# The first projection in four groups of 396 to 412 streamed columns, in another order of columns

## The chip, the core and the metric

The kernel runs on one core of a Trainium2 chip. The metric is the device time of one execution in microseconds, of which three runs are shown. Beside them stands one execution that the hardware profiler recorded. TensorE multiplies (PE in the profile; PEld is its loading of the stationary operand), ScalarE (ACT) rounds weights, moves results out of PSUM and computes exponentials and logarithms, VectorE (DVE) does the elementwise work, GpSimd (POOL) a few small steps, and SyncE (SP) issues the transfers from memory.

## What is computed

Two transformer blocks run over 256 tokens of width 1024, all in float32. The part that matters here is the start of the first block: a norm, the projection of the normed input to 2128 columns (and 3072 gate columns), and three kinds of attention that read those columns.

```python
u = _rmsnorm(h, norm_mix)
p = _split_columns(u @ w_in)          # q_a k_a v_a q_b k_b v_b q_idx k_idx w_idx q_c k_cmp ... g_c | g_merge
o_a = _stick_breaking(q_a, k_a, v_a)  # 4 heads of 64
o_b = _dsa_attention(_rope(q_b), _rope(k_b), v_b, _rope(q_idx), _rope(k_idx), w_idx)
o_c = _nsa_attention(_rope(q_c), _rope(k_cmp), v_cmp, _rope(k_sel), v_sel, _rope(k_win), v_win, sigmoid(g_c), ...)
merged = sum(sigmoid(g_merge)[i] * (o_i @ w_up[i]) for i in range(3))
h = h + merged @ w_out

def stick_breaking(z):                # per head, z = q k^T / 8, strictly below the diagonal
    log_1m = log_sigmoid(-z)
    suffix = reversed_cumsum(log_1m) - log_1m
    return exp(log_sigmoid(z) + suffix) @ v
```

Then follow a memory attention, a SwiGLU layer, and the second block with attention, retention and an MLP. None of them changes.

## The kernel before, in words

**Products.** A float32 product is made of three matmuls in a reduced form of float32: each operand is split into a rounded part (hi) and what is left (lo), and hi x hi, hi x lo and lo x hi are summed in PSUM. A contraction of 1024 is 8 slices of 128. All weights come in one stream of blocks, most of them 2048 values on each of 128 partitions. For each block SP loads it into one of four raw buffers (once the residue of the block four places ahead is made), ACT rounds it into one of three places of `sb_hi` (`round_block`, once PE is done with the block three places ahead), DVE subtracts to make `sb_lo` (`residue`), and PE multiplies (`take`).

**The first projection.** Blocks 0 and 1 (q_a, k_a) hold the weights still and stream the tokens (`by_feature`). Blocks 2 to 7 do it the other way round (`by_token`): for each half of the tokens (128) and each of 8 slices, three matmuls stream 256 weight columns, 48 matmuls in a block, both halves in one PSUM bank. Block 8 has the last 80 columns: 24 matmuls with the 80 columns held still and 256 tokens streamed; its result stands the wrong way round, so ACT copies it to `tail_t`, PE turns it in two transposes (`turn_tail`), and ACT copies it again. ACT writes results into `sb_proj`, scaled by the norm (L1412).

**Order of work.** `plan` writes one table of steps by hand. Each engine runs through the same table and does those steps that it has a part in, strictly in that order. `block(...)` adds the product of a block, then the rounding and residue of the two blocks ahead, then the evacuation of its result. With `between=` the product is cut in two halves, and other steps stand between them. A step on PE that needs a result of DVE waits in its place, and all that stands behind it on PE waits too.

**The head steps.** For each of the four stick-breaking heads there is `stick` (PE: scores; DVE: scaled and masked; ACT, for two heads at a time: absolute value, exponential, a table load, logarithm; DVE: the softplus, L1987), `suffix` (PE: the sum along the keys, which needs the softplus; DVE L1994; ACT: exponential L1549) and `pv_stick` (PE: times v). `rope1(g)` rotates columns on DVE in 8 instructions (L1950 to L1953), `turn_qk` transposes. `rstd_row` spreads the norm's factor over the partitions.

**Banks.** Results of the stream go in turn to PSUM banks 1 and 0 ("stream"). Before PE starts a result, `claim` waits until the bank's last content has been evacuated.

Of the kernel before, what the change touches and what calls it, by code (L numbers as in the profile page):

```python
# [21 lines left out]
ALU = mybir.AluOpType  # L22
# [87 lines left out]
def plan():  # L110

    blocks = [("proj", j) for j in range(9)] + [("gate", j) for j in range(12)]
# [39 lines left out]
    def block(*b, evac_now=True, ahead=True, hidden_first=False, between=None):  # L152
# [14 lines left out]
        if evac_now and b[0] not in ("up", "out", "mem_o", "ffn_out", "out2", "mlp_out"):  # L167
            evac(s)
# [77 lines left out]
    evac(2)  # L246
# [252 lines left out]
def weight_stream(w):  # L499
# [37 lines left out]
def two_blocks_kernel(nc, d, stream, consts_dram, out_dram):  # L537
# [4 lines left out]
    with ExitStack() as ctx:  # L542
# [101 lines left out]
        tail_t = summed[0:TAIL, 1, :]  # L644
# [62 lines left out]


# [47 lines left out]
        def _(pe):  # L756
# [118 lines left out]

            def take(s, cut=None):

                kind, j = blocks[s][0], blocks[s][-1]
                key = ("block", s)
                if kind == "proj2" and PROJ2_BLOCKS[j][0] == FF:  # L880
# [4 lines left out]
                elif kind == "proj" and j == 8:  # L885
                    ps = claim(key, "stream")
                    w_hi, w_lo = weights(s)
                    last = product(ps[0:TAIL, 0:T], [
                        (w_hi[:, k, :], w_lo[:, k, :], u_hi[:, k, :], u_lo[:, k, :]) for k in range(KD)])
                elif kind in ("proj", "proj2"):  # L890
                    n = 0 if kind == "proj" else 5
                    bank = j if kind == "proj" and j < 4 else j + 1 if kind == "proj2" and j < 3 else "stream"
                    ready = half_of_first if s == 1 else split_of(n) if j == (kind == "proj2") else None
                    if kind == "proj" and j < 2:
# [198 lines left out]
            def turn_tail():  # L1093

                ps = claim(("turn_tail",), "turn")
                wait_evacuated(pe, ("block", where["proj", 8]))
                for t in range(NT):
                    last = nc.tensor.transpose(ps[:, t * TAIL:t * TAIL + TAIL], tail_t[:, t * P:t * P + P],
                                               ident[0:TAIL, 0:TAIL])
                fill(last, ("turn_tail",))  # L1100

# [1395 lines left out]
```

## Time and profile before

| | |
|---|---|
| median of three runs | 752.87 us (751.75 to 753.01) |
| span of the profiled execution, first to last instruction | 750.7 us |
| PE busy | 742.7 us (99%) |
| DVE busy | 601.2 us (80%) |
| ACT busy | 376.9 us (50%) |
| matmul instructions recorded | 6374 |

A matmul's recorded duration has its way through the array in it, so that neighbours overlap. What it costs is the distance from its start to the start of the next. Lines of the timeline merge neighbours of one kind, "x2" says how many. A float32 matmul that isn't in the reduced form is recorded as two.

### The profile page before, as it was taken

The numbers are of one execution on the slowest core, as the hardware profiler recorded it, in microseconds if no ns is written. First come the engines' busy times: TensorE is split into PE (matmuls) and PEld (weight loads), VectorE is DVE, ScalarE is ACT, GpSimd is POOL, SyncE is SP. The second block draws the span as 40 slices with busy tenths as digits, with TensorE's granted clock in tenths as the row PEclk, the third lists the DMA queues.
The fourth block names the chain that finished last, engine by engine and source line by source line (L and its number), as shares of the span: only waits on it lengthen the run. The fifth ranks groups of instructions, "written<-read, shape, count | busy, mean of one in ns | idle before, by whom it ended". The sixth has DMA issues, their size and how long they took to land.

```text
span 750.7 us, 15016 instructions
## 1 busy us (share of the span) xinstructions
PE 742.7 (99%) x6374; PEld 733.2 (98%) x6374; DVE 601.2 (80%) x897; ACT 376.9 (50%) x506; POOL 30.6 (4%) x22
## 2 busy tenths in 40 slices
PE   8999999999999999999999999999999999999998
PEld 8999999999999999999999999999999999999997
DVE  5756889889897788998998788979787886687554
ACT  6558255745676533443434547356556553434330
POOL 0000000004000000000000000201110000000000
PEclk9999999999999999999999999999999999999999
DMA  9844373342843459999987336655344565678511
GB/s 336 319 153 146 110 275 113 113 139 108 309 174 115 169 173 389 334 349 329 335 306 271 138 127 230 224 174 219 103 173 139 205 224 173 224 281 301 201 58 56
DMA packets 24113, 156.07 MB, mean 208 GB/s; under 512 B 3568, under 2 KB 3696, under 8 KB 6000
## 3 DMA queue, kind: packets, MB, share of 16 engines
q1 hardware_dynamic: 24048, 155.13, 57.6%
q8 instruction: 50, 0.82, 0.4%
q14 instruction: 15, 0.12, 0.0%
HBM read 154.07 MB, written 1.05 MB: 207 GB/s over the span
## 4 chain that ended last, share of the span: by engine, by line
PE 95%; DVE 2%; ACT 1%; DMA 1%; issue 1%; DVEq 0%; SPq 0%
PE bank L786 17%; PE bank L787 16%; PE bank L788 16%; PE bank L867 9%; PE bank L870 9%; PE bank L869 9%; PE bank L794 3%; PE bank L796 3%; PE bank L797 3%; PE bank L1272 2%; PE bank L1239 1%; PE bank L1249 1%; PE bank L1169 1%; DMA sb_raw<-in_stream 1%; PE bank L1322 0%
## 5 line engine op out<-in xcount | busy, mean ns | idle before, releaser
L1742 DVE TENSOR_TENSOR sb_lo<-sb_raw,sb_hi 128x2048 fp32r<-128x2048 f32 (+1 forms) x116 | 261.7, 2259 | 74.5 <-ACT sb_hi L1406 74.1
L1406 ACT CAST sb_hi<-sb_raw 128x2048 fp32r<-128x2048 f32 (+1 forms) x116 | 217.8, 1882 | 100.7 <-PE bank L870 49.3
L786 PE MATMUL bank<-sb_u_hi,sb_hi 128*128 128x256 f32 (+2 forms) x696 | 195.4, 281 | 0.0
L787 PE MATMUL bank<-sb_u_lo,sb_hi 128*128 128x256 f32 (+2 forms) x696 | 192.7, 277 | 0.0
L788 PE MATMUL bank<-sb_u_hi,sb_lo 128*128 128x256 f32 (+2 forms) x696 | 192.6, 277 | 0.0
L786 PEld LDWEIGHTS bank<-sb_u_hi,sb_hi 128*128 128x128 f32 (+2 forms) x696 | 129.6, 186 | 3.0 <-issue 2.2
L787 PEld LDWEIGHTS bank<-sb_u_lo,sb_hi 128*128 128x128 f32 (+2 forms) x696 | 129.8, 186 | 0.3
L788 PEld LDWEIGHTS bank<-sb_u_hi,sb_lo 128*128 128x128 f32 (+2 forms) x696 | 129.7, 186 | 0.2
L867 PE MATMUL bank<-sb_hid_hi,sb_hi 128*128 128x256 f32 x432 | 119.3, 276 | 0.0
L870 PE MATMUL bank<-sb_hid_hi,sb_lo 128*128 128x256 f32 x432 | 119.2, 276 | 0.0
L869 PE MATMUL bank<-sb_hid_lo,sb_hi 128*128 128x256 f32 x432 | 119.2, 276 | 0.0
L786 PE MATMUL bank<-sb_hi,sb_u_hi 128*128 128x256 f32 x320 | 90.9, 284 | 0.0
L787 PE MATMUL bank<-sb_lo,sb_u_hi 128*128 128x256 f32 x320 | 88.8, 277 | 0.0
L788 PE MATMUL bank<-sb_hi,sb_u_lo 128*128 128x256 f32 x320 | 88.8, 277 | 0.0
L869 PEld LDWEIGHTS bank<-sb_hid_lo,sb_hi 128*128 128x128 f32 x432 | 81.1, 188 | 0.0
L867 PEld LDWEIGHTS bank<-sb_hid_hi,sb_hi 128*128 128x128 f32 x432 | 81.1, 188 | 0.0
L870 PEld LDWEIGHTS bank<-sb_hid_hi,sb_lo 128*128 128x128 f32 x432 | 81.1, 188 | 0.0
L786 PEld LDWEIGHTS bank<-sb_hi,sb_u_hi 128*128 128x128 f32 x320 | 60.3, 188 | 0.2
L787 PEld LDWEIGHTS bank<-sb_lo,sb_u_hi 128*128 128x128 f32 x320 | 60.2, 188 | 0.1
L788 PEld LDWEIGHTS bank<-sb_hi,sb_u_lo 128*128 128x128 f32 x320 | 60.1, 188 | 0.0
L2269 DVE SCALAR_TENSOR_TENSOR sb_raw<-sb_raw,sb_c_row 128x1024 f32<-128x1024 f32 x48 | 56.7, 1219 | 0.0
L1444 ACT ACTIVATE sb_act_out<-sb_masked 128x256 f32<-128x256 f32 x22 | 9.1, 418 | 81.8 <-DVE sb_masked L1822 81.8
(368 smaller groups left out, 1330.3 us busy)
## 6 DMA issues: line engine op xcount, KB each, us to landing
sb_raw<-in_stream SPq DMA_DIRECT2D x140, 1024.0 KB, 5.2
sb_raw<-in_stream SPq DMA_DIRECT2D x4, 256.0 KB, 6.6
sb_raw<-in_stream SPq DMA_DIRECT2D x2, 512.0 KB, 8.5
sb_mem_t<-in_mem SPq DMA_DIRECT2D x1, 1024.0 KB, 4.8
out<-sb_h SPq DMA_DIRECT2D x4, 256.0 KB, 2.2
sb_const<-in_constants SPq DMA_DIRECT2D x1, 830.0 KB, 10.8
sb_h<-in_x SPq DMA_DIRECT2D x1, 572.0 KB, 3.6
sb_h<-in_x SPq DMA_DIRECT2D x1, 512.0 KB, 7.0
```

Source lines behind the costliest of these rows:

```text
L786: nc.tensor.matmul(out, a_hi, b_hi, start=(i == 0), stop=False)
L787: nc.tensor.matmul(out, a_hi, b_lo, start=False, stop=False)
L788: last = nc.tensor.matmul(out, a_lo, b_hi, start=False, stop=(i == n - 1))
L794: nc.tensor.matmul(out, a_hi, b_hi, start=(k == 0 and i in opens), stop=False, skip_group_check=True)
L796: nc.tensor.matmul(out, a_hi, b_lo, start=False, stop=False, skip_group_check=True)
L797: last = nc.tensor.matmul(out, a_lo, b_hi, start=False, stop=(k == KD - 1), skip_group_check=True)
L867: nc.tensor.matmul(out, w_hi[:, k, f], x1, start=(first and k == m == 0), stop=False, skip_group_check=True)
L869: nc.tensor.matmul(out, w_hi[:, k, f], x2, start=False, stop=False, skip_group_check=True)
L870: last = nc.tensor.matmul(out, w_lo[:, k, f], x1, start=False, stop=last_one and k == 1, skip_group_check=True)
L1406: nc.scalar.copy(place(hi, s)[:, 0:n], x[:, 0:n]).then_inc(sem("hi_ready"), 1)
L1742: tt(place(lo, s)[:, 0:n], x[:, 0:n], f32(place(hi, s)[:, 0:n]), ALU.subtract) \
L2269: ins = stt(x[:, m, :], x[:, m, :], 1.0, c_row[:, :], ALU.mult, ALU.mult, accum_out=mod[:, 2 * j + m:2 * j + m + 1])
```

## The change

The columns of the first projection get another order: q_idx, k_idx, w_idx now stand ahead of q_b, k_b, v_b. Blocks 0 and 1 stay. The 1616 columns behind them, 512 to 2128, become four groups of 404, 404, 412 and 396 columns. A group comes in two blocks, each with half of the contraction (4 slices of 128) and all of its columns. A group holds two banks, one for each half of the tokens. Its first block opens the sums in both banks, its second one finishes them, and only then are they filled. So there are 10 projection blocks (8 of them in groups) instead of 9, each of the 8 with 24 matmuls of its group's width. The narrow block 8 and `turn_tail` are gone. A place in `sb_hi` and `sb_lo` holds the 4 slices 512 apart, so that rounding and residue write 4 x 404 and the like. Who waited for a block now waits for the group with the last column that it reads (`wait_columns`).

Steps move in the table too: suffix 0 now stands between the halves of block 6, rope1(0) behind block 7, and turn_qk 4 inside block 9.

```diff
+IN1_ORDER = ("QA", "KA", "VA", "QI", "KI", "WI", "QB", "KB", "VB", "QC", "KCMP", "VCMP", "KSEL", "VSEL", "KWIN",
+             "VWIN", "GC")
...
+GROUPS = {"proj": (512, 916, 1320, 1732, 2128)}
+GROUP_FROM = {"proj": 2}
+HK = KD // 2
...
-    blocks = [("proj", j) for j in range(9)] + [("gate", j) for j in range(12)]
+    blocks = [("proj", j) for j in range(10)] + [("gate", j) for j in range(12)]
...
-        if evac_now and b[0] not in ("up", "out", "mem_o", "ffn_out", "out2", "mlp_out"):
+        part_of_group = group_of(b)
+        if evac_now and (part_of_group is None or part_of_group[1]) and b[0] not in ("up", "out", "mem_o", "ffn_out", "out2", "mlp_out"):
             evac(s)
...
     block("proj", 2, evac_now=False)
     rstd(0)
-    evac(2)
     block("proj", 3, between=[("rstd_row", 0), ("evac", 0), ("evac", 1)])
     block("proj", 4)
     block("proj", 5)
     add("stick", 0), add("stick", 1)
     add("rope1", 1)
-    block("proj", 6)
-    steps([("suffix", 0), ("rope1", 0)])
+    block("proj", 6, between=[("suffix", 0)])
     block("proj", 7, between=[("suffix", 1)])
-    steps([("pv_stick", 0), ("stick", 2)])
-    block("proj", 8, ahead=False, evac_now=False)
+    steps([("rope1", 0), ("pv_stick", 0), ("stick", 2)])
+    block("proj", 8)
+    steps([("pv_stick", 1), ("stick", 3)])
+    block("proj", 9, ahead=False, evac_now=False, between=[("turn_qk", 4)])
     rounds(where["gate", 1])
-    evac(where["proj", 8])
-    steps([("pv_stick", 1), ("stick", 3), ("split", "gate", 1)])
-    block("gate", 0, ahead=False, between=[("turn_qk", 4), ("turn_tail",), ("rounds", "gate", 2)])
+    evac(where["proj", 9])
+    steps([("split", "gate", 1)])
+    block("gate", 0, ahead=False, between=[("rounds", "gate", 2)])
...
+            def group_product(s, cut):
...
+                def bank_of(t):
+                    if part:
+                        return banks[lease[keys[t]][0]]
+                    return claim(keys[t], 2 + t if g == 0 else "stream")
...
+                    for k in ks:
+                        x1, x2 = u_hi[:, HK * part + k, tok], u_lo[:, HK * part + k, tok]
+                        nc.tensor.matmul(out, x1, w_hi[:, k, :], start=(part == k == 0), stop=False,
+                                         skip_group_check=True)
+                        nc.tensor.matmul(out, x1, w_lo[:, k, :], start=False, stop=False, skip_group_check=True)
+                        last = nc.tensor.matmul(out, x2, w_hi[:, k, :], start=False,
+                                                stop=(part == 1 and k == HK - 1), skip_group_check=True)
...
+                if group_of(blocks[s]):
+                    g, _, c0, n = group_of(blocks[s])
+                    if kind == "proj":
+                        act.wait_ge(sem("rstd_ready"), RSTD_ORDER[0] + 1)
+                    for t in range(NT):
+                        ps = wait_filled(act, (kind, g, t))
+                        if kind == "proj":
+                            ins = nc.scalar.activation(proj[:, t, c0:c0 + n], ps[:, 0:n], ACT.Copy,
+                                                       scale=rstd[:, 0, t:t + 1])
...
-                c0, heads, last_block = ((QB, 5, 4), (QI, 5, 5), (QC, 5, 7), (KSEL, 2, 8))[g]
-                wait_evacuated(dve, ("turn_tail",) if last_block == 8 else ("block", where["proj", last_block]))
+                c0, heads, n = ((QB, 5, 320), (QI, 5, 320 + 4), (QC, 5, 320), (KSEL, 2, 256))[g]
+                wait_columns(dve, "proj", c0, n)
```

On PE, at the first head steps, before: the sticks of heads 0 and 1 write banks 5 and 4, then block 6 stands whole in bank 1 (48 matmuls, of which the first and last are shown), then suffix 0 in bank 7.

```order
L1110 MATMUL bank5<-sb_qk_t 128x256
L1111 MATMUL bank5<-sb_qk_t 128x128
L1110 MATMUL bank4<-sb_qk_t 128x256
L1111 MATMUL bank4<-sb_qk_t 128x128
L786 MATMUL bank1<-sb_hi,sb_u_hi 128x256
L787 MATMUL bank1<-sb_lo,sb_u_hi 128x256
...
L788 MATMUL bank1<-sb_hi,sb_u_lo 128x256
L1118 MATMUL bank7<-sb_prob_t,sb_const 128x128
L1119 MATMUL bank7<-sb_prob_t,sb_const 128x128
L1120 MATMUL bank7<-sb_prob_t,sb_const 128x128
L1121 MATMUL bank7<-sb_prob_t,sb_ones 128x128
```

The same place now: between the sticks and suffix 0 stand 12 matmuls of 412 columns, and the other 12 of the block come behind, in bank 0.

```order
L1191 MATMUL bank4<-sb_qk_t 128x256
L1192 MATMUL bank4<-sb_qk_t 128x128
L944 MATMUL bank1<-sb_hi,sb_u_hi 128x412
L946 MATMUL bank1<-sb_lo,sb_u_hi 128x412
L947 MATMUL bank1<-sb_hi,sb_u_lo 128x412
...
L1199 MATMUL bank7<-sb_prob_t,sb_const 128x128
L1200 MATMUL bank7<-sb_prob_t,sb_const 128x128
L1201 MATMUL bank7<-sb_prob_t,sb_const 128x128
L1202 MATMUL bank7<-sb_prob_t,sb_ones 128x128
L944 MATMUL bank0<-sb_hi,sb_u_hi 128x412
```

Suffix 0 has moved from 48 matmuls behind the sticks to 12.

On ACT, from the logarithms of heads 0 and 1 to the absolute value of head 2, before. `sb_prob<-sb_prob` behind the table load are the logarithms, `sb_hi<-sb_raw` is the rounding of a block, `sb_prob<-sb_masked` at L1549 the exponential of suffix 0 or 1, `sb_proj<-bank` the evacuation.

```order
L1544 ACTIVATE sb_prob<-sb_prob 128x384 x2
L1406 CAST sb_hi<-sb_raw 128x640
L1412 ACTIVATE sb_proj<-bank,sb_rstd 128x256 x2
L1549 ACT_TABLE_LOAD
L1549 ACTIVATE sb_prob<-sb_masked 128x384 x2
L1406 CAST sb_hi<-sb_raw 128x2048
L1412 ACTIVATE sb_proj<-bank,sb_rstd 128x256 x2
L1406 CAST sb_hi<-sb_raw 128x2048
L1450 COPY sb_summed<-bank 80x256
L1541 ACTIVATE sb_prob<-sb_masked 128x384
```

And now:

```order
L1621 ACTIVATE sb_prob<-sb_prob 128x384 x2
L1626 ACT_TABLE_LOAD
L1626 ACTIVATE sb_prob<-sb_masked 128x384
L1486 CAST sb_hi<-sb_raw 128x4x396
L1626 ACTIVATE sb_prob<-sb_masked 128x384
L1486 CAST sb_hi<-sb_raw 128x4x396
L1506 ACTIVATE sb_proj<-bank,sb_rstd 128x412 x2
L1486 CAST sb_hi<-sb_raw 128x2048
L1618 ACTIVATE sb_prob<-sb_masked 128x384
```

The rounding of blocks 8 and 9 has moved in between and behind the two exponentials, and the only evacuation here, of group 2, comes behind both. In the rows that follow on ACT, the evacuation of group 3 stands behind the steps of heads 2 and 3:

```order
L1621 ACT_TABLE_LOAD
L1621 ACTIVATE sb_prob<-sb_prob 128x384 x2
L1606 COPY sb_qk_t<-bank 128x512
L1486 CAST sb_hi<-sb_raw 128x2048
L1506 ACTIVATE sb_proj<-bank,sb_rstd 128x396 x2
L1486 CAST sb_hi<-sb_raw 128x2048
```

Before, the narrow block's copy to `sb_summed` (L1450 above) freed its bank ahead of those steps, and what stood here was the second copy of its 80 columns.

## Rows read from the trace of the kernel before

**Rows 1.** The page: busy time by engine, and the chain that ended last.

```profile
PE 742.7 (99%) x6374; PEld 733.2 (98%) x6374; DVE 601.2 (80%) x897; ACT 376.9 (50%) x506; POOL 30.6 (4%) x22
...
PE 95%; DVE 2%; ACT 1%; DMA 1%; issue 1%; DVEq 0%; SPq 0%
```

**Rows 2.** PE's longest wait: us in total, times, longest.

```profile
PE bank L794 <- DVE sb_lo L1728: 2.0, 1, 2.0
```

**Rows 3.** Timeline of PE, blocks 2 and 3: start us, us, operation.

```profile
19.88 0.28 PE L786 MATMUL bank<-sb_hi,sb_u_hi 128*128 128x256 f32 x1
...
25.54 0.50 PE L1053 MATMUL bank<-sb_ones,sb_summed 128*128 128x1 f32 x4
...
28.73 0.59 PE L1070 MATMUL bank<-sb_prob,sb_ones 128*128 128x256 f32 x2
...
29.28 0.28 PE L787 MATMUL bank<-sb_lo,sb_u_hi 128*128 128x256 f32 x1
```

**Rows 4.** Timeline of PE: first of 48 matmuls of 258 columns, and what follows.

```profile
593.13 0.28 PE L786 MATMUL bank<-sb_wide_hi,sb_hi 128*128 128x258 f32 x1
...
598.93 0.28 PE L867 MATMUL bank<-sb_hid_hi,sb_hi 128*128 128x256 f32 x1
```

**Rows 5.** Timeline of PE, from the first sticks to the third suffix step.

```profile
42.87 0.71 PE L1110 MATMUL bank<-sb_qk_t 64*128 64x256 f32 x4
...
43.73 0.38 PE L786 MATMUL bank<-sb_hi,sb_u_hi 128*128 128x256 f32 x1
...
49.28 0.38 PE L1118 MATMUL bank<-sb_prob_t,sb_const 128*128 128x128 f32 x2
...
56.63 0.33 PE L1131 MATMUL bank<-sb_proj,sb_prob 128*128 128x64 f32 x2
...
58.19 0.34 PE L786 MATMUL bank<-sb_u_hi,sb_hi 128*80 128x256 f32 x1
...
62.59 0.39 PE L786 MATMUL bank<-sb_u_hi,sb_hi 128*128 128x256 f32 x1
...
65.87 0.30 PE L1098 MATMUL bank<-sb_const,sb_summed 80*128 80x80 f32 x2
65.97 0.37 PE L786 MATMUL bank<-sb_u_hi,sb_hi 128*128 128x256 f32 x1
...
68.79 0.38 PE L1118 MATMUL bank<-sb_prob_t,sb_const 128*128 128x128 f32 x2
```

**Rows 6.** Timeline of ACT in the same stretch.

```profile
45.59 0.53 ACT L1541 ACTIVATE sb_prob<-sb_masked 128x384 f32<-128x384 f32 x1
...
48.83 0.71 ACT L1406 CAST sb_hi<-sb_raw 128x640 fp32r<-128x640 f32 x1
...
57.92 1.89 ACT L1406 CAST sb_hi<-sb_raw 128x2048 fp32r<-128x2048 f32 x1
59.71 0.83 ACT L1412 ACTIVATE sb_proj<-bank,sb_rstd 128x256 f32<-128x256 f32 x2
```

**Rows 7.** Timeline of DVE in the same stretch.

```profile
48.54 1.03 DVE L1987 SCALAR_TENSOR_TENSOR sb_prob_t<-sb_masked,sb_prob 128x384 f32<-128x384 f32 x2 [3.56 <-ACT sb_prob L1544]
49.48 0.48 DVE L1950 TENSOR_TENSOR sb_work<-sb_proj,sb_const 128x320 f32<-128x320 f32 x1
...
52.52 0.82 DVE L1742 TENSOR_TENSOR sb_lo<-sb_raw,sb_hi 128x640 fp32r<-128x640 f32 x1
53.27 0.55 DVE L1994 SCALAR_TENSOR_TENSOR sb_masked<-bank,sb_masked 128x384 f32<-128x384 f32 x1
...
59.84 2.29 DVE L1742 TENSOR_TENSOR sb_lo<-sb_raw,sb_hi 128x2048 fp32r<-128x2048 f32 x1 [2.39 <-ACT sb_hi L1406]
```

**Rows 8.** PE by windows: us, PE busy (x instructions), PEclk, DMA share, GB/s.

```profile
0.99:4.50 3.51, 3.51 (x16) 1.00 0.75 218
4.70:6.20 1.50, 1.50 (x16) 1.00 0.90 219
8.50:19.80 11.30, 11.30 (x96) 1.00 1.03 419
```

More of the change, by code:

```diff
@@ L884, in take @@
                         (w_hi[:, k, :], w_lo[:, k, :], u_hi[:, k, :], u_lo[:, k, :]) for k in range(KD)])
[L885 to L889, printed above, removed]
                 elif kind in ("proj", "proj2"):
[L891 to L894, printed above, removed]
+                    bank = j if kind == "proj" else j + 1 if j < 3 else "stream"
+                    ready = half_of_first if s == 1 else split_of(0 if kind == "proj" else 5) if j < 2 else None
+                    if kind == "proj":
                         last = by_feature(s, key, bank, u_hi, u_lo, ready)
@@ L1154, in turn_cmp @@
                 else:
-                    wait_evacuated(pe, ("block", where["proj", 7]))
+                    wait_columns(pe, "proj", VCMP, HD)
                 c = (KCMP, VCMP)[i]
@@ L1368, in turn_mixed @@
                 fill(last, ("turn_mixed", c))
-            run(dict(block=take, mem_v=mem_v, raw=raw_product, ssq_cols=ssq_cols, rstd_row=rstd_row, turn_qk=turn_qk, turn_tail=turn_tail, stick=stick, suffix=suffix,
+            run(dict(block=take, mem_v=mem_v, raw=raw_product, ssq_cols=ssq_cols, rstd_row=rstd_row, turn_qk=turn_qk, stick=stick, suffix=suffix,
                      pv_stick=pv_stick, index=index, turn_cmp=turn_cmp, cmp_product=cmp_product, cmp_kv=cmp_kv,
@@ L1402, in round_block @@
                 x = raw_ready(act, ("split", s))
-                n = KD * width(s) if width(s) != 256 else BLOCK
                 if s >= SPLIT:
                     wait_used(act, s - SPLIT)
-                nc.scalar.copy(place(hi, s)[:, 0:n], x[:, 0:n]).then_inc(sem("hi_ready"), 1)
-            def by_rstd(dst, both, n, key):
-                act.wait_ge(sem("rstd_ready"), RSTD_ORDER[n] + 1)
-                for t in range(NT):
-                    last = nc.scalar.activation(dst[:, t, :], both[:, t, :], ACT.Copy, scale=rstd[:, n, t:t + 1])
-                free(last, key)
+                nc.scalar.copy(slot(hi, s), in_rows(x, s)).then_inc(sem("hi_ready"), 1)
             def evac(s):
@@ L1448, in evac @@
                 both = ps[:, 0:2 * n].rearrange("p (t n) -> p t n", t=2)
-                if kind == "proj" and j == 8:
-                    free(nc.scalar.copy(tail_t[:, :], ps[0:TAIL, 0:T]), key)
-                elif kind == "proj":
-                    by_rstd(proj[:, :, 256 * j:256 * j + n], both, 0, key)
-                elif kind == "mem_q":
+                if kind == "mem_q":
                     free(nc.scalar.copy(qm_t, both), key)
@@ L1659, in _ @@
                  "u_norm": u_norm, "shift": shift, "evac_raw": evac_raw, "rstd_row": rstd_row, "c_act": c_act_,
[L1660 removed]
+                 "turn_qk": turn_qk, "stick": stick, "suffix": suffix, "gates_c": gates_c,
                  "cmp_hidden": cmp_hidden,
```

97 lines of the change are left out of this document (71 added, 26 removed).

## The prediction

> **What bounds the kernel now.** I read the page first. TensorE (PE) is busy for 742.7 of 750.7 us, and the chain that ended last is 95% PE [rows 1]. Then the waits of PE: the longest is 2.0 us, once, before the first matmul of the projection [rows 2]. So in the stretch that the change touches (20 to 69 us) PE issues without a pause, and the time is the sum of the distances between its matmuls. ScalarE (ACT) and VectorE (DVE) work behind it with free time. The change can pay only by taking time from PE's stream. It costs whatever it makes PE wait, and for that I read PE's timeline around the head steps and the timelines of ACT and DVE beside it.
>
> **What a matmul costs.** Block 2 is 48 matmuls of 256 columns from 19.88 to 25.54 us: 5.66 us, 117.9 ns each. Block 6 is 48 from 43.73 to 49.28 us: 5.55 us, less some 0.09 for the first one behind other work, which is 113.7 ns each [rows 3, 5]. Both are above the 106.7 ns that 256 columns take at 2.4 GHz, by 7 to 11 ns. With 258 columns 48 matmuls take 5.80 us, 120.8 ns [rows 4]: two columns more cost 7 ns. For 404 columns (168.3 ns of streaming) I bound the distance by 175 ns (7 ns on top) and 182 ns (13 on top, as the 258 columns have) and take 178. No matmul of such a width in this form stands in the trace.
> The Trainium skill (TensorE: Matmul & The Clock Gate, Back-to-back issue gap) gives N/2.4 + 2.5 ns. The rows differ from it: it gives 109.2 ns for 256 columns where 113.7 and 117.9 were measured. By it a matmul of 404 columns would be 170.8 ns, and the forecast would fall by 0.7 us.
>
> **Gain, part by part.** Before, blocks 2 to 8 are 312 matmuls of 256 columns; at 113.7 to 117.9 ns that is 35.5 to 36.8 us. Now 96 of 404, 48 of 412 and 48 of 396 columns stand there, 192 with 77,568 columns: at 178, 181 and 175 ns 34.2 us (ends 33.6 and 35.0). Both transposes of the narrow block go: 0.1 us, 65.87 to 65.97 [rows 5]. Sum: 1.3 to 2.7 us less on PE, some 1.7 us, if PE never waits.
> The smaller loads (1584 to 1648 values a partition for 2048), casts and residues lie beside PE. A cast of 640 columns takes 0.71 us and one of 2048 takes 1.89 [rows 6], so one of 1584 about 1.5 us. On DVE it is 0.82 and 2.29 us [rows 7], so about 1.8 us. ACT and DVE do less in all, and up to the head steps their order is the same but for one evacuation. I count nothing there: rstd_row starts 3.2 us after the first sums of block 2 are out in the old order [rows 3], and about 2.6 us in the new one, with ACT and DVE ahead by their shorter blocks.
>
> **Where the head steps now stand.** Call T0 the start of stick 0 and 1 on PE, 42.87 us before [rows 5]. Up to it the new stream is: 19.88, plus 24 x 0.178 = 4.27, plus 0.36 for the sums and 0.1 for the first matmul behind, plus 12 x 0.178 = 2.14, plus 0.44 for rstd_row (28.73 to the second matmul at 29.28, less one distance) [rows 3], plus 12 and then 48 x 0.178 = 10.68. That is T0 = 37.9 us.
> First wait. Before, 48 matmuls (5.55 us) stand between the sticks and suffix 0, and the softplus that suffix 0 needs is done by DVE at 48.54 + 0.52 = 49.06, that is T0 + 6.2; PE comes at T0 + 6.4 and just misses waiting [rows 5, 7]. Now suffix 0 stands between the halves of block 6, so there are only 12 matmuls: 0.86 for the sticks plus 0.1 plus 2.17 is T0 + 3.1. ACT and DVE are free at T0 before and after, so that chain keeps its length. **PE waits 3.1 us.** Behind the wait stand the rest of block 6, block 7, and all after.
> From there ACT and DVE go hand in hand, each step behind the last, by the order of the rows on both:
> softplus of both heads ends T0 + 6.7; rope1(1) 2.95 (49.57 to 52.52) to 9.65; suffix 0 on DVE 0.55 to 10.2; its exponential on ACT 0.5 (as every step on 384 elements) to 10.7; cast of block 8 1.5 to 12.2; its residue 1.8 to 14.0; suffix 1 0.55 to 14.5 (its product on PE lies at 11.5); exponential 0.5 to 15.0; cast of block 9 1.5 to 16.5; evacuation of the first half of group 2, 0.5 (two of 256 columns take 0.83) to 17.0 [rows 6, 7].
> PE meanwhile: suffix 0 at 6.25, plus 0.9, plus 24 x 0.181 is 11.5, suffix 1 0.9, 12 x 0.181 is 14.5, and pv_stick 0 with stick 2 takes 1.55 (56.63 to 58.19) [rows 5]: it reaches block 8 at T0 + 16.05. A group needs both stream banks, so block 8 must have bank 1, which is free at 17.0: **second wait, 0.9 us.**
> Third. DVE goes on: residue 9 to 18.3, rope1(0) 3.0 to 21.3, stick 2 0.6 (384 elements, as a suffix step) to 21.9, residue of gate 0 2.3 to 24.2, stick 3 0.6 to 24.8. ACT: from the second head's absolute value to the end of both logarithms 3.3 (45.59 to the next cast at 48.83, which overlaps a little) to 28.1, copy of turn_qk 4 0.6 (512 columns, an estimate from 0.42 for 256) to 28.7, cast of gate 1 1.85 to 30.5, and only then the first half of group 3, 0.45 to T0 + 31.0 [rows 6, 7]. Gate 0 claims that bank. PE: block 8 from 17.0, 4.3; head steps 1.65; block 9 with turn_qk 4 inside 4.75: T0 + 27.7. **Third wait, 3.3 us.** Before, gate 0 took the bank of block 7 and the evacuation of block 8 was short, so nobody waited: it started at 62.59 [rows 5].
> The sum: gate 0 starts at 37.9 + 31.0 = 68.9 and, with nothing inside it now, ends 5.55 later, at 74.45. Before, suffix 2 stands there at 68.79 [rows 5]. That is **5.65 us later**. (As a check: waits of 7.3 less a gain of 1.7.) From suffix 2 on all engines have the old order; DVE and ACT come to it less late than before, so PE follows without new waits and the delay stays to the end. The banks of a pair are swapped from gate 0 on; I count nothing for it.
>
> **Rivals.**
> A. The clock falls in the waits. PE has never stood for more than 2.0 us so far [rows 2], and behind that pause 96 matmuls ran at 118 ns each, the high level [rows 8]. At the start it was at the low level: 16 instructions in 3.51 us, then 16 in 1.50 [rows 8]. (The column reads 1.00 in both, the counts tell the levels, 1.2 and 2.4 GHz.) Such a fall costs up to half of 3.6 us, 1.8 us. After the first wait most of it is hidden, since block 8 waits for ACT anyway: some 0.5 us. After the third it is paid in full. Together 2 to 2.5 us: 760.5 to 761, up to 762.5. The skill's same page (Part 1: The HAM clock gate) says that an idle engine is put back to the low level and needs sustained work to rise; no row here shows a wait of 3 us.
> B. The other side, faster: the waits are not there, since the chain behind the sticks is shorter than PE's 12 matmuls with the sticks. It decides at T0 + 3.1: only if the softplus were out by then, and group 3 evacuated by T0 + 25, would the gain of 1.7 remain: 751.2 us. Against it: from the second head's absolute value at 45.59 to the cast behind the logarithms at 48.83 ACT needs 3.2 us by itself [rows 6].
> C. Only the first wait is whole, and the second and third are halved, because ACT or DVE run a step earlier than my row lengths say (patterns of 4 x 404 may cost other than 1616 in a row, to either side): 3 us less wait, 755.5.
> D. The wide matmul costs more: 190 ns. It delays T0 by 1.2 us, no more, for behind T0 the chain of ACT and DVE decides: 759.7.
>
> **How the numbers follow.** The forecast, all three waits at the full clock: 0.66. A 0.16, B 0.05, C 0.09, D 0.04. The median of the runs is 752.87, 2.2 above the profiled span; I add the 5.65 to it: 758.5 us (span 756.4). Row lengths good to 0.8 us over the chain, 0.5 for the width, and up to 1 us for which of its two paces (113 or 118 ns) PE takes in later stretches give 757.2 to 760.2 for the forecast alone. With A in full and the nearer half of C the range is 756.3 to 761.8. A difference under 0.2% (1.5 us) can't be told from none. Slower 0.93, same 0.02, faster 0.05.
>
> **What would show it.** PE's waits: one of some 3.1 us for DVE's softplus before suffix 0 at about 41.0 us, one of about 0.9 before block 8 and one of about 3.3 before gate 0, both for ACT's write of sb_proj. Distances of 175 to 182 ns between matmuls of 404 columns. T0 at 37.9, gate 0 at 68.9, the next suffix step at 74.4. With A, matmuls of 256 columns over 200 ns apart behind the third wait. It is wrong if PE goes through suffix 0 without a wait, or if ACT evacuates group 3 before T0 + 28.

## The result and the profile after

The change makes the kernel slower: 760.87 us median (759.2 to 762.0, four runs) against 752.35 (751.75 to 753.01, four runs), a ratio of 1.0109 with a 95% interval of 1.0095 to 1.0122: 7.1 to 9.2 us, 8.5 between the medians. The profiled execution has a span of 759.3 us, 8.6 above the one before. The forecast said 758.5 us, slower, with a range up to 761.8: the sign holds and the range holds the time, but the forecast's +5.65 us misses about a third of the loss. One execution among the experiments, the profiled one of e2_bank3, took 1247 us at a mean granted clock of 0.555 and is left out of every figure below.

The page of the changed kernel, the rows that answer to [rows 1]. PE has 122 matmul records fewer (312 matmuls became 192, and the two transposes are gone), is busy for 3.6 us longer, and the chain that ended last has more of DVE and ACT in it.

```profile
PE 746.3 (98%) x6252; PEld 735.3 (97%) x6252; DVE 602.0 (79%) x898; ACT 375.7 (49%) x500; POOL 30.6 (4%) x22
...
PE 92%; DVE 3%; ACT 2%; issue 1%; DMA 1%; SPq 0%; DVEq 0%; ACTq 0%
```

PE's longest waits, against [rows 2] (us in total, times, longest). Two of the three forecast waits are there: before suffix 0 for DVE's softplus, and before gate 0 for ACT's evacuation. The one before block 8 is not.

```profile
PE bank L1199 <- DVE sb_prob_t L2062: 2.9, 1, 2.9
PE bank L835 <- ACT sb_proj L1506: 2.6, 1, 2.6
PE bank L843 <- DVE sb_lo L1805: 1.6, 3, 0.9
```

PE's timeline (start us, us, operation), against [rows 3, 5]. In order: first matmul of block 2, the sticks (T0), the first of the 12 matmuls behind them, suffix 0, the rest of block 6, suffix 1, block 8, the last matmul of block 9, gate 0, suffix 2.

```profile
20.47 0.35 PE L944 MATMUL bank<-sb_hi,sb_u_hi 128*128 128x404 f32 x1
...
39.04 0.71 PE L1191 MATMUL bank<-sb_qk_t 64*128 64x256 f32 x4
...
39.90 0.46 PE L944 MATMUL bank<-sb_hi,sb_u_hi 128*128 128x412 f32 x1
...
45.31 0.49 PE L1199 MATMUL bank<-sb_prob_t,sb_const 128*128 128x128 f32 x2 [2.89 <-DVE sb_prob_t L2062]
...
46.23 0.45 PE L944 MATMUL bank<-sb_hi,sb_u_hi 128*128 128x412 f32 x1
...
52.38 0.38 PE L1199 MATMUL bank<-sb_prob_t,sb_const 128*128 128x128 f32 x2
...
57.09 0.45 PE L944 MATMUL bank<-sb_hi,sb_u_hi 128*128 128x396 f32 x1
...
67.76 0.34 PE L947 MATMUL bank<-sb_hi,sb_u_lo 128*128 128x396 f32 x1
70.73 0.58 PE L835 MATMUL bank<-sb_u_hi,sb_hi 128*128 128x256 f32 x1 [2.63 <-ACT sb_proj L1506]
...
77.87 0.38 PE L1199 MATMUL bank<-sb_prob_t,sb_const 128*128 128x128 f32 x2
```

Suffix 2 starts 9.08 us later than before (77.87 against 68.79). From there the delay changes little: it is 9.0 us at 78 us of the old trace, 8.2 at 260 and 8.7 from 454 us to the end. So the loss is made ahead of suffix 2, and the later stretches together give back some 0.4 us of it.

The granted clock by windows (us, PE busy, PEld, DVE, ACT, POOL, each with instructions, PEclk, DMA share, GB/s). PEclk of 0.5 is the lower of the two levels, 1.2 GHz.

```profile
46.20:49.60 3.40, 3.40 (x14) 3.30 (x13) 2.90 (x8) 0.51 (x2) 0.00 (x0) 0.55 0.00 0
49.95:52.30 2.35, 2.35 (x14) 2.33 (x13) 1.06 (x1) 1.25 (x1) 0.00 (x0) 1.00 0.00 0
70.70:73.80 3.10, 3.07 (x14) 3.07 (x15) 1.81 (x1) 3.08 (x3) 0.00 (x0) 0.50 0.21 34
73.90:77.70 3.80, 3.80 (x34) 3.80 (x34) 0.00 (x0) 0.35 (x1) 0.00 (x0) 1.00 0.62 246
```

The clock was down behind both waits. Fourteen matmuls took 3.4 us in the first window where as many take 2.35 in the next, and behind gate 0's start 14 take as long as 27 would at full speed (some 115 ns apart, as behind 73.9 us). From gate 0 to suffix 2 it is 7.14 us in place of the forecast 5.55.

Last the two engines that hold up gate 0: ACT and DVE (in brackets the idle time before a row, and who ended it), against [rows 6, 7].

```profile
64.58 0.53 ACT L1618 ACTIVATE sb_prob<-sb_masked 128x384 f32<-128x384 f32 x1 [2.06 <-DVEq L2059]
...
65.68 1.28 ACT L1621 ACT_TABLE_LOAD   x1
66.98 0.94 ACT L1621 ACTIVATE sb_prob<-sb_prob 128x384 f32<-128x384 f32 x2
67.82 0.57 ACT L1606 COPY sb_qk_t<-bank 128x512 f32<-128x512 f32 x1
68.29 1.90 ACT L1486 CAST sb_hi<-sb_raw 128x2048 fp32r<-128x2048 f32 x1
70.09 1.08 ACT L1506 ACTIVATE sb_proj<-bank,sb_rstd 128x396 f32<-128x396 f32 x2
```

```profile
53.47 0.56 DVE L2069 SCALAR_TENSOR_TENSOR sb_masked<-bank,sb_masked 128x384 f32<-128x384 f32 x1 [0.43 <-PE bank L1202]
...
61.39 2.29 DVE L1818 TENSOR_TENSOR sb_lo<-sb_raw,sb_hi 128x2048 fp32r<-128x2048 f32 x1
63.60 0.55 DVE L2057 SCALAR_TENSOR_TENSOR sb_masked<-bank,sb_const 128x384 f32<-128x384 f32 x1
```

Read it backwards from gate 0 at 70.73: the first evacuation of 396 columns at 70.09, behind the rounding of gate 1, the copy, the logarithms with their table load, the absolute value at 64.58; that one waited for DVE's scaling of head 3 at 63.60, and this stood behind a residue of 2048 values. These are the steps of the forecast, in its order. The 0.43 in the first DVE row is new: DVE waits for PE's suffix 1, which the low clock has made late.

### The profile page after: what moved, and what is told of

The parts are those of the page before. It is cut to its first block, busy times and chain, and to the rows that moved or that the text cites. A ratio compares the mean times of both kernels' runs of the same rounds, so it can differ in the third digit from the quotient of the medians.

```text
span 759.3 us, 14763 instructions
## 1 busy us (share of the span) xinstructions
PE 746.3 (98%) x6252; PEld 735.3 (97%) x6252; DVE 602.0 (79%) x898; ACT 375.7 (49%) x500; POOL 30.6 (4%) x22
## 3 DMA queue, kind: packets, MB, share of 16 engines
HBM read 154.07 MB, written 1.05 MB: 204 GB/s over the span
## 4 chain that ended last, share of the span: by engine, by line
PE 92%; DVE 3%; ACT 2%; issue 1%; DMA 1%; SPq 0%; DVEq 0%; ACTq 0%
PE bank L835 15%; PE bank L837 15%; PE bank L836 15%; PE bank L918 9%; PE bank L921 9%; PE bank L920 9%; PE bank L843 3%; PE bank L845 3%; PE bank L846 3%; PE bank L1353 2%; PE bank L1320 1%; PE bank L1330 1%; PE bank L946 1%; PE bank L944 1%; PE bank L947 1%
## 5 line engine op out<-in xcount | busy, mean ns | idle before, releaser
L1818 DVE TENSOR_TENSOR sb_lo<-sb_raw,sb_hi 128x2048 fp32r<-128x2048 f32 (+4 forms) x117 | 261.9, 2241 | 76.5 <-ACT sb_hi L1486 76.0
L1486 ACT CAST sb_hi<-sb_raw 128x2048 fp32r<-128x2048 f32 (+4 forms) x117 | 217.9, 1867 | 100.7 <-PE bank L921 47.3
L835 PE MATMUL bank<-sb_u_hi,sb_hi 128*128 128x256 f32 (+1 forms) x688 | 193.8, 282 | 2.6 <-ACT sb_proj L1506 2.6
L836 PE MATMUL bank<-sb_u_lo,sb_hi 128*128 128x256 f32 (+1 forms) x688 | 191.1, 278 | 0.0
L837 PE MATMUL bank<-sb_u_hi,sb_lo 128*128 128x256 f32 (+1 forms) x688 | 191.0, 278 | 0.0
L835 PEld LDWEIGHTS bank<-sb_u_hi,sb_hi 128*128 128x128 f32 (+1 forms) x688 | 129.1, 188 | 5.6 <-ACT sb_proj L1506 3.0
L836 PEld LDWEIGHTS bank<-sb_u_lo,sb_hi 128*128 128x128 f32 (+1 forms) x688 | 129.3, 188 | 0.4
L837 PEld LDWEIGHTS bank<-sb_u_hi,sb_lo 128*128 128x128 f32 (+1 forms) x688 | 129.2, 188 | 0.2
L835 PE MATMUL bank<-sb_hi,sb_u_hi 128*128 128x256 f32 x224 | 63.9, 285 | 0.0
L836 PE MATMUL bank<-sb_lo,sb_u_hi 128*128 128x256 f32 x224 | 62.3, 278 | 0.0
```

The lines of the kernel that those rows point to most:

```text
L835: nc.tensor.matmul(out, a_hi, b_hi, start=(i == 0), stop=False)
L836: nc.tensor.matmul(out, a_hi, b_lo, start=False, stop=False)
L837: last = nc.tensor.matmul(out, a_lo, b_hi, start=False, stop=(i == n - 1))
L1486: nc.scalar.copy(slot(hi, s), in_rows(x, s)).then_inc(sem("hi_ready"), 1)
L1818: tt(slot(lo, s), in_rows(x, s), f32(slot(hi, s)), ALU.subtract).then_inc(sem("lo_ready"), 1)
```

## The experiments

All but e6_old_suffix start from the changed kernel. T0 is the start of the sticks of heads 0 and 1 on PE. The theory: two waits of PE, made by the new places of suffix 0 and of group 3's evacuation, with the clock falling behind them, are the loss. The rivals: the wide matmuls or the banks themselves cost it; or something else holds PE anyway.

### e1_warm: the waits filled with matmuls

```diff
                 elif kind == "gate":
+                    if j == 0 and not cut:
+                        pe.wait_ge(freed[3], uses[3])
+                        stay_warm(banks[3], 16)
...
             def suffix(hd):
 
+                ps = claim(("suffix", hd), "turn")
+                stay_warm(ps, 13 if hd == 0 else 0)
                 pe.wait_ge(sem("softplus_ready"), hd + 1)
-                ps = claim(("suffix", hd), "turn")
```

`stay_warm(ps, n)` is a helper that the kernel has already: n matmuls of a tile of ones, whose result nobody reads.

> Edit: PE fills both long waits with matmuls on constants, 13 ahead of suffix 0 (into the bank that suffix 0 then writes) and 16 ahead of gate 0 (into bank 3, which is free); 128 columns in plain float32, 0.22 us each by the rows of the suffix steps. The waits themselves stay. Theory (the clock falls because PE stands for 2.6 to 2.9 us): the granted clock is 1.00 at 46 to 50 us and behind gate 0's start, the 412-column matmuls behind suffix 0 are 189 ns apart at once; suffix 1 comes early enough for DVE (0.43 us less on the chain to gate 0), gate 0 is 1.6 us shorter. Sum -2.0 us: 758.9 us against 760.9, gate 0 at T0 + 31.3. Rival (the slow stretches have another cause, such as the banks or the width): both stay, 760.9. Rival (the clock explains all that the forecast missed): 758.5 or less.

Measured: 759.38 us (759.21 to 760.0), 1.5 us less than the changed kernel. PE's timeline: the filler (suffix 0 follows at 45.43), then block 8, gate 0 and suffix 2.

```profile
42.38 3.06 PE L822 MATMUL bank<-sb_ones 128*128 128x128 f32 x26
...
56.23 0.42 PE L944 MATMUL bank<-sb_hi,sb_u_hi 128*128 128x396 f32 x1 [0.49 <-ACT sb_proj L1510]
...
70.54 0.36 PE L835 MATMUL bank<-sb_u_hi,sb_hi 128*128 128x256 f32 x1
...
76.28 0.38 PE L1203 MATMUL bank<-sb_prob_t,sb_const 128*128 128x128 f32 x2
```

The window behind suffix 0 that read 0.55 in the changed kernel, and the one behind gate 0's start:

```profile
46.30:49.70 3.40, 3.40 (x21) 3.38 (x20) 2.91 (x8) 0.51 (x2) 0.00 (x0) 1.00 0.00 0
70.60:73.70 3.10, 3.10 (x29) 3.10 (x28) 1.50 (x1) 3.08 (x3) 0.00 (x0) 1.00 0.22 34
```

The granted clock is 1.00 in both, and its mean is 0.999 or 1.0 in all four runs, where the changed kernel's lie between 0.993 and 0.998. T0 is 39.15 here, so gate 0 stands at T0 + 31.39 (31.3 expected), and suffix 2 5.74 us behind it in place of 7.14. Suffix 2 is 1.7 us earlier as counted from T0. (It could be 0.2 us more: gate 0 follows the first row of its evacuation on ACT by 0.87 us here and by 0.64 in the changed kernel, because the last of the 16 filler matmuls are still running.) So the fall of the clock is real and costs 1.7 to 1.9 us, but it is the smaller part: with it gone the kernel is still 6.9 us behind the one before (759.38 against 752.47 measured beside it). And the wait before block 8, which the forecast had and the changed kernel hadn't, is here with 0.5 us: at the full clock PE is early enough to meet it.

### e2_bank3 and e2b_bank3: gate 0 in a free bank

```diff
-                    last = by_feature(s, key, "stream", u_hi, u_lo, None, cut)
+                    last = by_feature(s, key, 3 if j == 0 else "stream", u_hi, u_lo, None, cut)
```

> Edit: gate 0 takes bank 3, which is free here, in place of bank 1. Theory (gate 0 waits for the evacuation of group 3 alone): no wait before gate 0, which starts right behind block 9, at T0 + 28.7 in place of 31.7, and no low clock behind it (1.6 us). Sum -4.6 us: 756.3 us. The first wait and the first fall of the clock stay. Rival (the weights of gate 0 are as late as the bank, so that the wait only changes its name): 760.9. Rival (the chain of ACT and DVE gives the delay back behind suffix 2): 757.5 to 759.

> The kernel of e2_bank3 once more, for a profile at the usual clock. Expected as there: wait of 2.9 us before suffix 0 with the clock at half for 3.4 us behind it, gate 0 at T0 + 28.7 without a wait, clock 1.00 behind it, suffix 2 5.7 us later.

Measured: 756.5 us (755.68 to 757.93, four runs) in the first and 755.47 (one run) in the second, which is the same kernel and whose profile is used here; 756.3 was expected. PE's waits and its timeline at block 8, gate 0 and suffix 2:

```profile
PE bank L1199 <- DVE sb_prob_t L2062: 2.9, 1, 2.9
```

```profile
55.61 0.42 PE L944 MATMUL bank<-sb_hi,sb_u_hi 128*128 128x396 f32 x1 [0.49 <-ACT sb_proj L1506]
...
66.25 0.34 PE L947 MATMUL bank<-sb_hi,sb_u_lo 128*128 128x396 f32 x1
66.43 0.28 PE L835 MATMUL bank<-sb_u_hi,sb_hi 128*128 128x256 f32 x1
...
71.89 0.38 PE L1199 MATMUL bank<-sb_prob_t,sb_const 128*128 128x128 f32 x2
```

Gate 0 follows the last matmul of block 9 without a pause, at T0 + 27.90, and suffix 2 comes 5.46 us later at the full clock. Its weights were ready, so nothing but the evacuation of group 3 had held it. The surprise is the first wait: again 2.9 us, but the window behind it shows the full clock, against what was expected. (That is also why gate 0 stands 0.8 us ahead of the T0 + 28.7 expected.)

```profile
44.80:48.20 3.40, 3.40 (x21) 3.38 (x22) 3.26 (x10) 1.07 (x1) 0.00 (x0) 1.00 0.00 0
```

Twenty-one matmuls in 3.4 us, where the changed kernel had 14. The same wait in the same place is followed by a fall in one execution and by none in another. The other runs of this kernel fit: the mean clock is 0.998 in three (756.05 to 757.93 us) and 1.0 in the fourth (755.68).

### e3_suffix: suffix 0 and 1 back behind more matmuls

```diff
-    block("proj", 6, between=[("suffix", 0)])
-    block("proj", 7, between=[("suffix", 1)])
-    steps([("rope1", 0), ("pv_stick", 0), ("stick", 2)])
+    block("proj", 6)
+    block("proj", 7, between=[("suffix", 0)])
+    steps([("suffix", 1), ("rope1", 0), ("pv_stick", 0), ("stick", 2)])
```

> Edit: suffix 0 and suffix 1 stand where they stood before, counted in halves of blocks: block 6 whole, suffix 0 between the halves of block 7, suffix 1 behind it. So 36 wide matmuls stand between the sticks and suffix 0 (T0 + 7.8) and DVE's softplus is out at T0 + 6.2. Theory: the wait of 2.9 us and the first fall of the clock go, but the chain of ACT and DVE still sets gate 0: small waits of about 0.8 us before pv_stick 0 and 0.5 before block 8, gate 0 at T0 + 29.1 in place of 31.7 behind a wait of some 3.7 us with a low clock behind it. Sum -2.6 us: 758.3 us. Rival (each wait adds by itself, so that the first one's 2.9 us and its fall of 1.7 come off in full): 756.3.

Measured: 758.44 us (758.11 to 759.62), 758.3 expected. PE's waits (rows of other lines left out):

```profile
PE bank L835 <- ACT sb_proj L1506: 3.7, 1, 3.7
...
PE bank L1212 <- ACT sb_prob L1626: 0.6, 1, 0.6
...
PE bank L944 <- ACT sb_proj L1506: 0.3, 1, 0.3
```

The wait of 2.9 us is gone, and 1.1 us of it comes back before gate 0, which now waits 3.7 in place of 2.6, with the clock at 0.50 from 68.7 to 72.0 us. Gate 0 starts at T0 + 29.22 (29.1 expected). The rival that takes each wait for itself (756.3) is 2.1 us off: the waits lie on one chain of ACT and DVE, and a wait that is taken away ahead is partly waited out behind. The loss shrinks by 2.4 us, to 758.44.

### e4_both: both

The edits of e2_bank3 and e3_suffix together.

> Edit: both, suffix 0 and 1 back behind more matmuls and gate 0 in bank 3. Theory: no wait over 1 us on PE behind T0, no low clock, gate 0 at T0 + 25.4, suffix 2 5.7 later: -7.8 us, 753.1 us, which is 0.7 above the kernel before: the blocks themselves then gain next to nothing, since a matmul of 404 columns costs 183 ns and not 178. Rival (the groups do gain the 1.7 us of the forecast once nothing waits): 750.7. Rival (another wait appears): over 755.

Measured: 752.93 us (751.71 to 754.37, ten runs), 753.1 expected; ratio to the kernel before 1.0006 (0.9997 to 1.0016). PE at the sticks, gate 0 and suffix 2:

```profile
38.10 0.71 PE L1191 MATMUL bank<-sb_qk_t 64*128 64x256 f32 x4
...
63.45 0.28 PE L835 MATMUL bank<-sb_u_hi,sb_hi 128*128 128x256 f32 x1
...
68.91 0.38 PE L1199 MATMUL bank<-sb_prob_t,sb_const 128*128 128x128 f32 x2
```

Gate 0 at T0 + 25.35 (25.4 expected). Two small edits, one of the order and one of a bank, without touching the groups, take back 7.9 of the 8.5 us between the medians; one by one they took back 4.4 and 2.4. That refutes the rival that the wide matmuls or the groups themselves are the loss: they are about neutral.

### e5_width: 400 and 416 columns

```diff
-GROUPS = {"proj": (512, 916, 1320, 1732, 2128)}
+GROUPS = {"proj": (512, 912, 1312, 1728, 2128)}
```

> Edit: the four groups have 400, 400, 416 and 400 columns in place of 404, 404, 412 and 396, all multiples of 16; the sum stays 1616. Measured so far: 256 columns 113.3 or 117.8 ns apart, 258 columns 120.8, 396 columns 180, 404 columns 183.3, 412 columns 189. Reading A (the price goes up in steps of 16 columns, 7.1 ns each, so that 258 costs as 272 and 404 as 416): 400 columns 177 ns, 416 columns 184; the 96 matmuls from block 2 to the sticks take 0.6 us less, T0 17.95 us behind the first wide matmul in place of 18.57. Reading B (streaming at 2.4 GHz plus some 15 to 17 ns, whatever the width): 400 columns 181.7, 416 columns 189 to 191, T0 18.4 behind. Behind T0 the chain of ACT and DVE decides, so the time falls by no more than T0 does: A 760.3 us, B 760.8.

Measured: 760.25 us (759.59 to 760.71), too near to the changed kernel to say more than "no great gain". The trace decides: 400 columns stand 183.3 ns apart (mean) and 416 columns 187, and T0 stands 18.56 us behind the first wide matmul. 400 columns cost as much as 404, and 416 less than the 189 of 412 in the changed kernel. Steps of 16 columns (reading A, 177 and 184 ns) are refuted; reading B is nearer, but for 416 columns too high.

### e6_old_suffix: the kernel before, with this step alone

```diff
-    block("proj", 6)
-    steps([("suffix", 0), ("rope1", 0)])
+    block("proj", 6, between=[("suffix", 0)])
+    steps([("rope1", 0)])
```

> Edit: the kernel before, with one step of the change alone: suffix 0 stands between the halves of block 6 (24 matmuls of 256 columns behind the sticks in place of 48). Theory: PE reaches suffix 0 at T0 + 3.7, DVE's softplus is out at T0 + 6.2, so PE waits 2.5 us, and suffix 1 and all behind come 2.6 us later. If the clock falls behind this wait too, 3.4 us at half speed cost another 1.7. Sum +2.6 us at the full clock, +4.3 with the fall: 755.1 or 756.8 us against 752.5. Rival (the wait is hidden, since something later than suffix 0 holds PE anyway): 752.5.

Measured: 756.62 us (755.01 to 758.03), ratio 1.0046 (1.003 to 1.0062), some 3.5 us; 755.1 was expected without a fall of the clock and 756.8 with one. PE's longest wait, suffix 0 on its timeline, and the clock in the two windows behind it:

```profile
PE bank L1118 <- DVE sb_prob_t L1987: 2.4, 1, 2.4
```

```profile
43.08 0.71 PE L1110 MATMUL bank<-sb_qk_t 64*128 64x256 f32 x4
...
49.36 0.79 PE L1118 MATMUL bank<-sb_prob_t,sb_const 128*128 128x128 f32 x2 [2.43 <-DVE sb_prob_t L1987]
```

```profile
49.00:52.30 3.30, 2.94 (x14) 2.94 (x15) 3.20 (x10) 1.41 (x2) 0.00 (x0) 0.50 0.00 0
52.40:56.00 3.60, 3.60 (x34) 3.60 (x33) 2.35 (x6) 1.99 (x4) 0.00 (x0) 1.00 0.01 2
```

With no group and no wide matmul in it, the old kernel shows the same wait for the same releaser, suffix 0 at T0 + 6.28, and the same fall of the clock. Moving one step of the table costs 3.5 us by itself, the fall included (mean clock 0.998 in three of the five runs, 1.0 in two).

### e7_rope: without the small waits too

The edits of e4_both, and on DVE rope1(1) behind suffix 0:

```diff
-    add("rope1", 1)
     block("proj", 6)
-    block("proj", 7, between=[("suffix", 0)])
+    block("proj", 7, between=[("suffix", 0), ("rope1", 1)])
```

> Edit: as e4_both (suffixes back, gate 0 in bank 3), and rope1(1) of DVE stands behind suffix 0 instead of ahead of it. Theory: DVE does suffix 0 at T0 + 9.4 in place of 11.5, so that its exponential, the rounding of block 9 and the evacuation of group 2 on ACT come 2 us earlier; the two small waits of e4_both (0.6 us before pv_stick 0, 0.3 us before block 8, and the starts behind them) go, gate 0 at T0 + 24.2 in place of 25.35. Sum -1.1 us against e4_both's 752.9: 751.8 us, 0.6 under the kernel before, hardly to be told from it. Rival (the 1.7 us that the forecast gave the groups are there once nothing waits): 750.7. Rival (rope1(1) now holds up what stands behind it, the second exponential or turn_qk 4): 752.9 or more.

Measured: 751.93 us (751.02 to 752.21, eleven runs) against 753.0 of the kernel before on the same chip (sixteen runs), ratio 0.9984 (0.9975 to 0.9993). The two small waits are gone, and gate 0 starts at T0 + 24.21 (24.2 expected). PE at the first wide matmul, the sticks, gate 0 and suffix 2:

```profile
20.24 0.35 PE L943 MATMUL bank<-sb_hi,sb_u_hi 128*128 128x404 f32 x1
...
38.81 0.71 PE L1190 MATMUL bank<-sb_qk_t 64*128 64x256 f32 x4
...
63.02 0.28 PE L834 MATMUL bank<-sb_u_hi,sb_hi 128*128 128x256 f32 x1
...
68.48 0.38 PE L1198 MATMUL bank<-sb_prob_t,sb_const 128*128 128x128 f32 x2
```

From block 2 to suffix 2 it is 48.24 us, against 48.91 before (19.88 to 68.79) [rows 3, 5]. That 0.67 us is what the groups are worth where PE never waits: a gain, but well short of the 1.7 that the forecast granted them. By the times it is 1.1 us between the medians, 0.5 to 1.9 by the interval.

### e8_probe: what a width costs

```diff
+            probe = claim(("probe",), 7)
+            def paced(n, at, pitch, which="split"):
+                for i in range(24):
+                    k, part = i // 3 % 4, i % 3
+                    w = (lo if part == 1 else hi)[:, at + k * pitch:at + k * pitch + n]
+                    x = (u_lo if part == 2 else u_hi)[:, k, 0:P]
...
+                    nc.tensor.matmul(probe[:, 0:n], x, w, start=i == 0, stop=i == 23, skip_group_check=True)
...
+            for n in (128, 192, 256, 258, 272, 320, 384, 396, 400, 404, 412, 416, 448, 480, 512):
+                paced(n, 96, 512)
...
```

> Edit: behind the last product of the changed kernel PE multiplies on into a bank that nobody reads, with the operands of a group (24 matmuls of one width in a row, hi x hi, hi x lo, lo x hi, slices 512 apart, places from column 96): widths of 128 to 512. Then 256 and 404 columns from column 0, with slices as far apart as they are wide, and with one slice and one held operand again and again. ACT, DVE and the transfers are idle there. It is 21 x 24 matmuls longer; read are the distances. Reading 1 (the wide matmul's price is its own): 396, 404 and 412 columns stand 180, 183 and 189 ns apart here too, 15 to 17 ns above streaming, 256 columns 113 or 118. Reading 2 (the price comes from other engines' work beside PE): 404 columns fall to 175 or less. Reading 3 (from the slices 512 apart or from the start at column 96): 404 columns from column 0, or 404 apart, are under 178.

PE's timeline, the first of the 24 matmuls of four widths. From one start to the next are 24 distances: 4.32 us for 396 columns is 180.0 ns each, 4.40 us for 404 is 183.3.

```profile
777.84 0.34 PE L1468 MATMUL bank<-sb_hi,sb_u_hi 128*128 128x396 f32 x1
...
782.16 0.34 PE L1468 MATMUL bank<-sb_hi,sb_u_hi 128*128 128x400 f32 x1
...
786.56 0.35 PE L1468 MATMUL bank<-sb_hi,sb_u_hi 128*128 128x404 f32 x1
...
790.96 0.35 PE L1468 MATMUL bank<-sb_hi,sb_u_hi 128*128 128x412 f32 x1
```

Mean distances over each row of 24 (the largest and smallest left out), beside streaming at 2.4 GHz. 256 columns were measured four times; in the first row the distances from the fifth on are 113 and 114 ns (mean 113.4). The rows of 272 and 448 columns are left out.

| columns | ns apart | streaming | ns per column |
|---|---|---|---|
| 128 | 111.5 | 53.3 | 0.87 |
| 192 | 111.9 | 80.0 | 0.58 |
| 256 | 114.3 (once) or 117.7 (three times) | 106.7 | 0.446 or 0.460 |
| 258 | 120.7 | 107.5 | 0.468 |
| 320 | 146.5 | 133.3 | 0.458 |
| 384 | 176.7 | 160.0 | 0.460 |
| 396 | 180.0 | 165.0 | 0.455 |
| 400 | 183.4 | 166.7 | 0.458 |
| 404 | 183.2 | 168.3 | 0.453 |
| 412 | 186.7 | 171.7 | 0.453 |
| 416 | 186.7 | 173.3 | 0.449 |
| 480 | 216.2 | 200.0 | 0.450 |
| 512 | 233.3 | 213.3 | 0.456 |

With all other engines idle, 396 and 404 columns cost what they cost in the kernel (180 and 183 ns). So reading 1 holds; that 412 columns have 186.7 here and 189 there stays open. Above streaming stand 8 to 10% from 320 columns on: 13 ns at 320 and 416 columns, 15 at 396 to 412, 17 at 384, 20 at 512. The rows decide neither for a fixed amount nor for a fixed share; 400 and 404 columns cost the same, and so do 412 and 416. At 128 and 192 columns the distance is 112 ns, whatever the width. Starting at column 0, slices 404 apart, or one operand again and again change nothing to speak of at 404 columns (183.3 to 184.0).
A column costs as much at 404 as at 256. Leaving 312 matmuls for 192 wider ones saves nothing for being fewer, only the 2,304 columns by which the sum is smaller, some 1.05 us at 0.455 ns (an estimate).

### e9_again: the changed kernel once more

> The changed kernel again, unedited, for a second profile. Theory: waits of 2.9 us before suffix 0 and 2.5 to 3 us before gate 0, each with a chance of a fall of the clock (1.7 us of stream each) and not with certainty: in e2b_bank3 the same first wait was followed by full speed. T0 18.57 us behind the first wide matmul, gate 0 at T0 + 31.3 (no first fall) to 31.7 (with it). Times between 758.5 (no fall) and 762, the median near 760.8; the mean clock of each run tells the falls (0.998 for one, 0.996 for two), and time goes with it at about 1.7 us per fall.

Measured: 761.62 us (760.96 to 762.79), near 760.8 expected. PE's two long waits have their old sizes, 2.9 and 2.6 us. Both were followed by the low clock again, and gate 0 stands at T0 + 31.69 as before. Over the eight runs of this kernel in both comparisons the mean clock goes from 0.993 (762.0 and 762.79 us) through 0.995 and 0.996 (760.6 to 762.0) to 0.998 (759.2). A fall is the rule in this kernel, not a certainty.

## Why the prediction was right in sign and short in size

**The first wait: right.** Forecast from T0 + 3.1 to T0 + 6.25, measured suffix 0 at T0 + 6.27 behind 2.9 us. e6_old_suffix shows the same wait in the old kernel.

**The chain of ACT and DVE to gate 0: right in kind, 0.7 us short.** Forecast T0 + 31.0, measured 31.69. 0.43 us is DVE's wait for suffix 1 on PE, which the low clock delayed; it is absent in e1_warm, where gate 0 stands at T0 + 31.39. The forecast also counted nothing between DVE's end of head 3 (63.60 + 0.55 = 64.15) and ACT's start on it (64.58), another 0.43 us. Steps that were a little shorter than forecast make good the difference.

**The second wait: not there.** The forecast let PE reach block 8 at T0 + 16.05 and the bank come free at 17.0. PE came at T0 + 18.05, since suffix 1 stood at T0 + 13.34 and not 11.5. In e1_warm and e2b_bank3, where the clock stayed up, the wait is there with 0.5 us. It changes nothing for gate 0, which ACT and DVE hold up in the changed kernel.

**The third wait: right, 2.6 us in place of 3.3**, because PE itself came 1.2 us later than forecast (T0 + 28.9) and the bank only 0.7. e2_bank3 shows that the bank alone is its cause.

**T0: 39.04 in place of 37.9.** Two terms. The start of block 2 was taken as 19.88 from the trace of before; it was 20.47 in this execution, and between 19.20 and 20.58 in the profiles of the other kernels with the same start. That is scatter and no effect of the change. The other 0.55 us is a mis-sized term: from block 2 to the sticks it is 18.57 us in place of 18.02, since 96 matmuls of 404 columns stand 183.3 and not 178 ns apart. The term that was mis-sized is the surcharge on streaming: bounded by what 256 and 258 columns have, 7 and 13 ns [rows 3, 4], it measured 15 ns at 404 columns. So even the gain that the forecast granted the groups, 1.7 us, was too high; e7_rope finds 0.67. By the rule of the Trainium skill that the forecast weighed (TensorE: Matmul & The Clock Gate, Back-to-back issue gap), which the section gives for an isolated matmul, the estimate for 404 columns is 170.8 ns, further off than either bound; the measurement decides.

**The clock: rival A is what happened.** It was given a chance of 0.16 against 0.66 for the forecast, and named 760.5 to 761 us; 760.87 was measured. Its two prices fit as well: "some 0.5 us" behind the first wait (0.43), and up to 1.8 behind the third (7.14 less 5.55 is 1.6). The mechanism was seen and the odds were wrong. The odds leaned on the one long wait that the old trace shows, 2.0 us with full speed behind it [rows 2, 8]. Waits of 2.4 to 3.7 us, not filled with matmuls, were followed by the low level in nine of the eleven cases that were profiled (twice each in the changed kernel, in e9_again and in e8_probe; once in e3_suffix, in e5_width's first and in e6_old_suffix's; not in e2b_bank3, nor behind e5_width's second of 2.5 us). That rival A's number was hit so closely is in part luck: in the profile the width and the scatter of the start add 1.14 us that it had not counted, the later stretches take 0.4 off, and the median before came out 0.5 us below the one that the forecast was added to.

**The sum at suffix 2** (9.08 us measured): 5.65 of the forecast, 0.59 for the start of block 2, 0.55 for the width, 0.69 for the chain, 1.59 for the low clock in gate 0, together 9.07. That it stays to the end was right within 0.4 us.

**The other rivals.** B (no waits, faster) is refuted by the rows of waits. C (the second and third wait halved by a shorter chain) is wrong: the chain was longer, and what took away the second wait and shortened the third was PE's own delay. D's direction was right, its 190 ns too high.

## What to carry to other kernels

A step that waits for a chain of other engines needs as many matmuls ahead of it as the chain is long. Moving one such step too near to its producer cost 3.5 us in the old kernel (e6_old_suffix), and moving it and its neighbour back won 2.4 in the new one (e3_suffix), both more than the whole regrouping could bring. The remedy was to move them back and to give the next block a bank that nobody was late for. Compare widths by time per column: here everything from 256 to 512 columns costs 0.44 to 0.47 ns a column, so by these rows wider tiles pay only for matmuls that were clearly under 256 columns. Price a forecast wait on PE of the size seen here, 2.4 to 3.7 us, with a likely fall of its clock behind it.

## What the runs showed of the hardware

- In this reduced form of float32 the distance between matmuls is 8 to 10% above streaming at 2.4 GHz for 320 columns and more (146 ns at 320, 183 at 404, 187 at 416, 233 at 512), and 112 ns at both 128 and 192 columns (e8_probe). 256 columns come in two paces, 113.4 ns (behind the first four distances of the row) and 117.7 ns, both in e8_probe with the other engines idle. What chooses between them is open.
- The same wait of 2.9 us before suffix 0 was followed by the lower clock in four of the five profiles in which it stands (46.2 to 49.6 us: 0.55) and by the full clock in one (44.8 to 48.2: 1.00). What decides it wasn't tested. The Trainium skill (TensorE: Matmul & The Clock Gate, Part 1: The HAM clock gate) puts an idle engine back to the low level; the four profiles agree, and the fifth shows that this idle time needn't be enough.
- With thirteen matmuls on constants in the first wait and sixteen in the second the clock stayed up in the profile of e1_warm, and its mean was 0.999 or more in all four runs. The thirteen cost nothing (suffix 0 at T0 + 6.28 against 6.27), since they lay inside the wait; the sixteen ran over by some 0.2 us.
